# Part of the output projection moved in among the last attention heads

## The chip, the cores and the metric

The kernel runs on one core of a Trainium2 chip. The time is the device time of one execution, in microseconds (us). TensorE (PE) does the matrix products, VectorE (DVE) and ScalarE (ACT) the element-wise work, GpSimd (POOL) some setup and a few transfers, and SyncE (SP) starts nearly all loads of weights. Each engine runs its own instructions in order; they meet at semaphores.

## What is computed

Two transformer blocks in a row, 256 tokens of width 2048, all in float32. The change is in the first block, between its attention and its first residual:

```python
h = rmsnorm(x, pre_mix_g[l])
proj = h @ w_in[l]
...
o_a = swa_sink_attention(...)        # 16 heads of 64: the sliding half
o_b = forgetting_attention(...)      # 16 heads of 64: the forgetting half
o_a = rmsnorm(o_a.reshape(B, S, D_SWA), grp_swa_g[l])
o_b = rmsnorm(o_b.reshape(B, S, D_FOX), grp_fox_g[l])
mix = jnp.concatenate([o_a, o_b], axis=-1) @ w_out[l]
x = x + rmsnorm(mix, post_mix_g[l])
```

The two halves of the attention output are normalised apart. So the first 1024 rows of `w_out` need only the sliding heads, and the other 1024 rows need the forgetting heads.

## The kernel before

**Weights.** Every weight matrix is cut into groups of 512 output columns, and a group into pieces of 256 rows by 512 columns (`PLAN` lists the groups and how many pieces each has). SP loads a piece into one of four slots of `raw`. A function `split` on ACT copies it rounded into `w_hi`, then `split` on DVE writes the difference into `w_lo`. TensorE multiplies each piece three times (`three`: high by high, high by low, low by high), so a piece costs 12 matmuls of 512 columns, or 24 of 256. `group` on ACT and DVE splits three pieces ahead of the one that TensorE multiplies.

**Banks.** PSUM has eight banks of 512 columns. The sums of a group lie in banks 0 and 1 or in banks 2 and 3, in turn; banks 4 to 7 ("upper") serve the attention heads. `banks_free` counts the emptied ones.

**Heads.** There are 32 heads: 0 to 15 sliding, 16 to 31 forgetting. They run as a pipeline of steps `head(i)`. In step i TensorE computes the scores of head i, turns the probabilities of head i-2 and multiplies those of head i-3 with the values. DVE adds the bias and takes the row maximum of head i, then the reciprocal for head i-1, then scales the output of head i-3 into `work`. ACT copies the turned probabilities of head i-2 and takes the exponentials of head i. Steps 0 to 23 lie between the pieces of groups 3 to 8 of the input projection. Steps 24 to 34 follow alone:

```python
for i in range(24, 2 * NH + 3):
    head(i)
stay_warm(4, 16)
phase(1, work, 6, 4)
with pe.Fori(0, 2) as i:
    for e in range(2):
        group(GROUP["w_out"][e], "tok", i, 16, first=1 if e == 0 else None)
```

**From heads to projection.** After the last step the squares of the two halves are summed, and their roots taken together on ACT (`root`, which needs another function table than the exponentials). DVE scales the first 1536 columns of `work` and ACT the other 512. Then `phase(1)` turns `work` into columns: 32 transposes on TensorE in eight quads, a rounded copy per 128 rows on ACT (`hT_hi`) and the difference on DVE (`hT_lo`). Sixteen idle matmuls (`stay_warm`) stand ahead. Only then come the four groups of the output projection, 8 pieces each. `w_hi` has 64 spare columns: pieces whose weights are the stationary operand (input projection, `w_up`) are put 16 columns further in (`PIECE_AT`); the first three of `w_up` are not, since the loop over `w_out` puts them in its own place.

## Time and profile before

| what | value |
|---|---|
| three runs | 1681.15, 1681.36 and 1685.89 us; median 1681.36 |
| the profiled execution | 1682.97 us |
| its span, first to last instruction | 1680.9 us |
| TensorE busy | 1644.2 us, 98% |
| VectorE busy | 1007.8 us, 60% |
| ScalarE busy | 877.3 us, 52% |
| steps 24 to 34, first to last matmul | 250.82 to 271.79 us from the start |
| output projection, first matmul to the end of the last | 281.07 to 368.24 us |

The profiled execution is 1.61 us above the median, and 2.07 us of its time lie outside the span. All places in the trace below are in us from the start of the span.

### The profile page before, as it was taken

The numbers are of one execution on the slowest core, as the hardware profiler recorded it, in microseconds if no ns is written. First come the engines' busy times: TensorE is split into PE (matmuls) and PEld (weight loads), VectorE is DVE, ScalarE is ACT, GpSimd is POOL, SyncE is SP. The second block draws the span as 40 slices with busy tenths as digits, with TensorE's granted clock in tenths as the row PEclk, the third lists the DMA queues.
The fourth block names the chain that finished last, engine by engine and source line by source line (L and its number), as shares of the span: only waits on it lengthen the run. The fifth ranks groups of instructions, "written<-read, shape, count | busy, mean of one in ns | idle before, by whom it ended". The sixth has DMA issues, their size and how long they took to land.

```text
span 1680.9 us, 28894 instructions
## 1 busy us (share of the span) xinstructions
PE 1644.2 (98%) x11198; PEld 1501.7 (89%) x11198; DVE 1007.8 (60%) x1437; ACT 877.3 (52%) x1264; POOL 21.8 (1%) x46
## 2 busy tenths in 40 slices
PE   8999999999999999999999999989999999999996
PEld 8989998879999999999998888878998888898885
DVE  5566667556666666666664444473666455776565
ACT  6355557446555554554453444354434695655455
POOL 3000000000000000000000000010000000000000
PEclk9999999999999999999999999999999999999999
DMA  7654541554666666666665665556566547655641
GB/s 232 203 157 140 162 139 45 193 163 153 192 189 188 187 193 200 200 199 190 197 213 177 200 205 189 175 149 169 166 180 176 162 147 245 185 176 176 195 155 64
DMA packets 154574, 295.09 MB, mean 176 GB/s; under 512 B 13428, under 2 KB 15624, under 8 KB 153592
## 3 DMA queue, kind: packets, MB, share of 16 engines
q1 hardware_dynamic: 153512, 289.76, 55.7%
q0 software_dynamic: 944, 4.14, 0.7%
q8 instruction: 59, 0.97, 0.2%
q14 instruction: 27, 0.22, 0.0%
q10 hardware_dynamic: 32, 0.01, 0.0%
HBM read 291.51 MB, written 2.10 MB: 175 GB/s over the span
## 4 chain that ended last, share of the span: by engine, by line
PE 95%; DVE 2%; ACT 1%; issue 0%; DMA 0%; ACTq 0%; SPq 0%; DVEq 0%
PE bank L1487 29%; PE bank L1489 29%; PE bank L1488 29%; PE upper L1629 1%; PE upper L1632 1%; ACT junk L522 1%; PE upper L1543 1%; PE bank L1543 1%; PE upper L1646 1%; PE upper L1762 1%; DMA x_tok<-in_x 0%; PE upper L1659 0%; PE upper L1660 0%; PE upper L1806 0%; PE upper L1658 0%
## 5 line engine op out<-in xcount | busy, mean ns | idle before, releaser
L891 DVE TENSOR_TENSOR w_lo<-raw,w_hi 128x1024 fp32r<-128x1024 f32 (+1 forms) x548 | 654.5, 1209 | 530.5 <-ACT w_hi L464 529.0
L464 ACT ACTIVATE w_hi<-raw 128x1024 fp32r<-128x1024 f32 (+1 forms) x548 | 568.3, 1049 | 573.4 <-PE bank L1489 567.4
L1487 PE MATMUL bank<-hT_hi,w_hi 128*128 128x256 f32 x2272 | 632.0, 278 | 1.3 <-DVE hT_lo L922 1.3
L1488 PE MATMUL bank<-hT_lo,w_hi 128*128 128x256 f32 x2272 | 629.1, 277 | 0.0
L1489 PE MATMUL bank<-hT_hi,w_lo 128*128 128x256 f32 x2272 | 629.0, 277 | 0.0
L1487 PEld LDWEIGHTS bank<-hT_hi,w_hi 128*128 128x128 f32 x2272 | 427.0, 188 | 2.6 <-issue 1.7
L1488 PEld LDWEIGHTS bank<-hT_lo,w_hi 128*128 128x128 f32 x2272 | 427.5, 188 | 0.0
L1489 PEld LDWEIGHTS bank<-hT_hi,w_lo 128*128 128x128 f32 x2272 | 426.8, 188 | 0.0
L1487 PE MATMUL bank<-w_hi,hT_hi 128*128 128x512 f32 x672 | 264.7, 394 | 0.0
L1489 PE MATMUL bank<-w_hi,hT_lo 128*128 128x512 f32 x672 | 261.8, 390 | 0.0
L1488 PE MATMUL bank<-w_lo,hT_hi 128*128 128x512 f32 x672 | 261.5, 389 | 0.0
L1489 PEld LDWEIGHTS bank<-w_hi,hT_lo 128*128 128x128 f32 x672 | 126.1, 188 | 26.5
L1487 PEld LDWEIGHTS bank<-w_hi,hT_hi 128*128 128x128 f32 x672 | 126.2, 188 | 25.9 <-issue 0.3
L1488 PEld LDWEIGHTS bank<-w_lo,hT_hi 128*128 128x128 f32 x672 | 126.3, 188 | 25.5
L1489 PE MATMUL bank<-w_hi,g_lo 128*128 128x512 f32 x352 | 137.0, 389 | 0.0
L1488 PE MATMUL bank<-w_lo,g_hi 128*128 128x512 f32 x352 | 137.0, 389 | 0.0
L1487 PE MATMUL bank<-w_hi,g_hi 128*128 128x512 f32 x352 | 136.9, 389 | 0.0
L1487 PEld LDWEIGHTS bank<-w_hi,g_hi 128*128 128x128 f32 x352 | 66.1, 188 | 13.8
L1488 PEld LDWEIGHTS bank<-w_lo,g_hi 128*128 128x128 f32 x352 | 66.1, 188 | 13.8
L1489 PEld LDWEIGHTS bank<-w_hi,g_lo 128*128 128x128 f32 x352 | 66.1, 188 | 13.5
L1128 DVE SCALAR_TENSOR_TENSOR cv_gate<-bank,coef,cv_gate 128x255 f32<-128x255 f32 (+1 forms) x88 | 36.4, 476 | 27.3 <-ACT cv_gate L653 26.9
L1128 DVE SCALAR_TENSOR_TENSOR cv_val<-bank,coef,cv_val 128x255 f32<-128x255 f32 (+1 forms) x88 | 36.4, 476 | 26.5 <-ACT cv_val L653 26.1
(347 smaller groups left out, 1080.1 us busy)
## 6 DMA issues: line engine op xcount, KB each, us to landing
raw<-in_w_in SPq DMA_DIRECT2D x180, 512.0 KB, 3.8
raw<-in_w_up SPq DMA_DIRECT2D x176, 512.0 KB, 4.5
raw<-in_w_down SPq DMA_DIRECT2D x80, 512.0 KB, 4.6
raw<-in_w_out SPq DMA_DIRECT2D x64, 512.0 KB, 4.3
raw<-in_w_xkv SPq DMA_DIRECT2D x16, 512.0 KB, 4.5
raw<-in_w_down SPq DMA_DIRECT2D x16, 256.0 KB, 3.1
raw<-in_w_xq SPq DMA_DIRECT2D x8, 512.0 KB, 3.9
raw<-in_w_xo SPq DMA_DIRECT2D x8, 512.0 KB, 4.6
```

The lines of the kernel that those rows point to most:

```text
L464: act.activation(w_hi[:, s, at:at + n], raw[:, s, 0:n], ACT.Copy).then_inc(hi_ready, 1)
L522: act.activation(jk, src, ACT.Square, accum_out=col).then_inc(done, 1)
L891: dve.tensor_tensor(w_lo[:, s, at:at + n], raw[:, s, 0:n], w_hi[:, s, at:at + n].bitcast(F32), ALU.subtract).then_inc(lo_ready, 1)
L1128: ins = dve.scalar_tensor_tensor(out=cv[:, ft, back:S], in0=ps[:, 0:S - back], scalar=coef[:, e, tap, ft:ft + 1], in1=cv[:, ft, back:S], o ...
L1487: pe.matmul(o, l_hi, r_hi, start=start, stop=False, skip_group_check=True)
L1488: pe.matmul(o, l_hi, r_lo, start=False, stop=False, skip_group_check=True)
L1489: return pe.matmul(o, l_lo, r_hi, start=False, stop=stop, skip_group_check=True)
L1543: ins = pe.transpose(bank[pair_bank(n, q)][:, c % 2 * S + b * P:c % 2 * S + (b + 1) * P], src[:, b, c * P:(c + 1) * P], ident[:, :])
L1629: ins = pe.matmul(o[:, lo:hi], qaT[:, h // 2, b * P:(b + 1) * P], ka2[:, h // 8, h % 2, 0:n], start=True, stop=True)
L1632: pe.matmul(o[:, lo:hi], qbT[:, h // 2, b * P:(b + 1) * P], kbT[:, h // 2, h % 2, 0:n], start=True, stop=False)
L1646: ins = pe.transpose(bank[6][:, c * P:(c + 1) * P], probs[:, s, c * P:(c + 1) * P], ident[:, :])
L1762: ins = pe.matmul(bank[4 + 2 * b + h % 2][:, t * P:(t + 1) * P], src[po:po + HD, 1, t, b * P:(b + 1) * P], src[po:po + HD, 0, t, qb * P:(q ...
```

## The change

The four groups of `w_out` are taken apart. Rows 0 to 1023 of the first two groups (`w_out_a`, 4 pieces each, eight in all) run early: one piece after each of the steps 25, 26, 27, 28, 31 and 33 (`EARLY`), and two after step 34. Their sums stay in banks 0 to 3. Then rows 1024 to 2047 of the same two groups (`w_out_b`) are added to them, and the last two groups (`w_out`) follow whole.

For this the sliding half is normalised by itself. Step 22 gets the root on ACT, step 23 the scaling of 1024 columns on DVE, and after step 24 comes the first half of the transposes (`out_phase`), with its copies into new tensors `sT_hi` and `sT_lo`. The forgetting half has the second `out_phase`, after the early pieces. The 16 `stay_warm` matmuls go. The gain that is needed from the first emptied bank on (`mix_gain`) lies in a new place that is free only after the scores of the last head, and its load waits for them. The loops over `w_out` are written out, and the first three pieces of `w_up` now lie 16 columns in, like the rest of `w_up`.

```diff
-    + [("w_out", 8)] * 4 + [("w_up", 8)] * 22 + [("w_down", 24)] * 4
+    + [("w_out_a", 4)] * 2 + [("w_out_b", 4)] * 2 + [("w_out", 8)] * 2 + [("w_up", 8)] * 22 + [("w_down", 24)] * 4
...
+EARLY = (25, 26, 27, 28, 31, 33)
...
-for _name, _before in (("w_up", "w_out"), ("w_down", "w_up"), ("xq", "w_out2")):
+for _name, _before in (("w_down", "w_up"), ("xq", "w_out2")):
...
+    if n == 1:
+        return [p, p + 1, 2 - p, 3 - p, 4, 5, 6, 7][q]
...
+        _, sT_hi, sT_lo = region([("sT_after", [P, NB, D], F32), ("sT_hi", [P, 8, S], F32R), ("sT_lo", [P, 8, S], F32R)])
+        _, mix_gain = region([("mix_gain_after", [P, 11776], F32), ("mix_gain", [P, D], F32)])
...
-            with sp.Fori(0, 2) as i:
-                for e in range(2):
-                    group(A["w_out"][0], i * (2 * W) + e * W, GROUP["w_out"][e], i, 16)
+            w_out = A["w_out"][0]
+            for e in range(2):
+                group(w_out[0:D // 2, :], e * W, GROUP["w_out_a"][e], pieces=(2,) * 4)
+            for e in range(2):
+                group(w_out[D // 2:D, :], e * W, GROUP["w_out_b"][e], pieces=(2,) * 4)
+            for e in range(2):
+                group(w_out, (2 + e) * W, GROUP["w_out"][e])
...
+            pool.wait_ge(scores_done, 2 * NH)
             pool.dma_start(mix_gain[:, :], A["post_mix_g"][0].partition_broadcast(P)).then_inc(gain_loaded, 16)
...
+                if i == 22:
+                    act.wait_ge(swa_mean, 1)
+                    act.activation(half_stat(0), half_stat(0), ACT.Sqrt).then_inc(swa_root, 1)
...
+            early = FIRST_PIECE[GROUP["w_out_a"][0]]
             for i in range(24, 2 * NH + 3):
                 head(i)
-            root(2, 1, mean_ready, root_ready, 4)
+                if i == 24:
+                    out_phase(range(8))
+                if i in EARLY:
+                    split(early + EARLY.index(i) + SLOTS - 1)
+            act.wait_ge(mean_ready, 2)
+            act.activation(half_stat(1), half_stat(1), ACT.Sqrt).then_inc(root_ready, 1)
             scale_part(work, work, 2, head_factor)
-            phase(1)
+            out_phase(range(8, KC))
+            for j in (6, 7):
+                split(early + j + SLOTS - 1)
...
+                if i == 22:
+                    dve.wait_ge(squares, 4)
+                    dve.tensor_scalar(half_stat(0), half_stat(0), 1.0 / D_SWA, EPS, ALU.mult, ALU.add).then_inc(swa_mean, 1)
+                if i == 23:
+                    dve.wait_ge(swa_root, 1)
+                    dve.reciprocal(half_stat(0), half_stat(0)).then_inc(swa_rstd, 1)
+                    dve.wait_ge(swa_rstd, 1)
+                    for c in range(2):
+                        for b in range(NB):
+                            dve.tensor_scalar(work[:, b, c * W:(c + 1) * W], work[:, b, c * W:(c + 1) * W], head_factor(b, c), None,
+                                              ALU.mult).then_inc(scaled, 1)
...
+            def out_piece(g, j, k0):
+
+                u, pair = FIRST_PIECE[g] + j, 2 * (g % 2)
+                pe.wait_ge(lo_ready, u + 1)
+                hi, lo = wide(w_hi, u % SLOTS, 2, W), wide(w_lo, u % SLOTS, 2, W)
+                for c in range(2):
+                    k = k0 + 2 * j + c
+                    pe.wait_ge(loT_done, KC + max(k + 1, 4))
+                    a_hi, a_lo = out_t(k)
+                    for b in range(NB):
+                        ins = three(bank[pair + b][:, :], a_hi[:, b * P:(b + 1) * P], a_lo[:, b * P:(b + 1) * P],
+                                    hi[:, c, :], lo[:, c, :], k == 0, k == KC - 1)
+                ins.then_inc(mm_done, 1)
+
             for i in range(24, 2 * NH + 3):
                 head(i)
-            stay_warm(4, 16)
-            phase(1, work, 6, 4)
-            with pe.Fori(0, 2) as i:
-                for e in range(2):
-                    group(GROUP["w_out"][e], "tok", i, 16, first=1 if e == 0 else None)
+                if i == 24:
+                    out_phase(range(4))
+                if i in EARLY:
+                    j = EARLY.index(i)
+                    out_piece(GROUP["w_out_a"][j // 4], j % 4, 0)
+            for j in (6, 7):
+                out_piece(GROUP["w_out_a"][j // 4], j % 4, 0)
+            out_phase(range(4, 8))
+            for g in GROUP["w_out_b"]:
+                for j in range(4):
+                    out_piece(g, j, 8)
+            for g in GROUP["w_out"]:
+                pe.wait_ge(banks_free, evacuated(g - 2))
+                for j in range(8):
+                    out_piece(g, j, 0)
```

How instructions move on TensorE, at step 24. Before, `head(25)` (its scores, `upper<-kbT,qbT`) followed the values of `head(24)` (`upper<-vb,probsT`) directly:

```order
L1658 MATMUL upper<-vb,probsT 128x64 [waits out_done,probsT_copied]
L1659 MATMUL upper<-vb,probsT 128x64
L1660 MATMUL upper<-vb,probsT 128x64
L1632 MATMUL upper<-kbT,qbT 128x128 [waits biased_done]
L1635 MATMUL upper<-cT2,eye2 128x128
L1632 MATMUL upper<-kbT,qbT 128x256
```

Now 16 transposes stand between them, of the sliding half, into banks 2, 3, 0 and 1:

```order
L1736 MATMUL upper<-vb,probsT 128x64 [waits out_done,probsT_copied]
L1737 MATMUL upper<-vb,probsT 128x64
L1738 MATMUL upper<-vb,probsT 128x64
L1786 MATMUL bank2<-ident,work 128x128 [waits scaled,banks_free]
L1786 MATMUL bank2<-ident,work 128x128 x3
L1786 MATMUL bank3<-ident,work 128x128 x4
L1786 MATMUL bank0<-ident,work 128x128 [waits scaled]
L1786 MATMUL bank0<-ident,work 128x128 x3
L1786 MATMUL bank1<-ident,work 128x128 x4
L1710 MATMUL upper<-kbT,qbT 128x128 [waits biased_done]
```

They wait for `scaled`, the scaling on DVE. Behind the next step stands the first early piece, which waits for `loT_done`, the copies of those transposes on DVE:

```order
L1736 MATMUL upper<-vb,probsT 128x64 [waits out_done,probsT_copied]
L1737 MATMUL upper<-vb,probsT 128x64
L1738 MATMUL upper<-vb,probsT 128x64
L1565 MATMUL bank2<-w_hi,sT_hi 128x512 [waits loT_done,lo_ready]
L1566 MATMUL bank2<-w_lo,sT_hi 128x512
L1567 MATMUL bank2<-w_hi,sT_lo 128x512
```

On ScalarE, the end of step 22 and the start of step 23: two loads of the function table and a root (`stat<-stat`, waits `swa_mean`) are new here; ahead of them are the exponentials of head 22, between them a split and the two copies of group 8 (`kbT`):

```order
L586 ACTIVATE probs,stat<-biased,stat 128x256
L604 ACT_TABLE_LOAD
L604 ACTIVATE stat<-stat 128x2 [waits swa_mean]
L489 ACTIVATE w_hi<-raw 128x1024 [waits mm_done,raw_loaded2]
L634 ACTIVATE kbT<-bank0 64x2x256 [waits k_cleared,mm_done]
L635 ACTIVATE kbT<-bank0 64x2x256
L571 ACTIVATE probsT<-upper 128x384 [waits pv_done,probs_T]
L583 ACT_TABLE_LOAD [waits recip_done,probs_T]
L583 ACTIVATE stat<-stat 128x2 [waits neg_max]
```

So the split now stands behind a table load and the root. The second table load waits for nothing new; the exponential behind it waits for `neg_max`, as before.

On VectorE, the end of step 23: the reciprocal that waits for `swa_root` and the four scalings behind it are new, between the output of head 20 and the bias of head 24:

```order
L1056 RECIPROCAL stat<-stat 128x2 [waits out_done,exp_done]
L1061 TENSOR_TENSOR work<-upper,stat 128x2x64 [waits recip_done,pv_done]
L1076 RECIPROCAL stat<-stat 128x2 [waits swa_root]
L1080 TENSOR_SCALAR work<-work,stat 128x512 [waits swa_rstd]
L1080 TENSOR_SCALAR work<-work,stat 128x512 x3
L1033 SCALAR_TENSOR_TENSOR biased<-upper,c8,foxm 128x128 [waits exp_done,scores_done]
```

## Rows read from the trace of the kernel before

**Rows 1.** The page: busy time of each engine

```profile
PE 1644.2 (98%) x11198; PEld 1501.7 (89%) x11198; DVE 1007.8 (60%) x1437; ACT 877.3 (52%) x1264; POOL 21.8 (1%) x46
```

**Rows 2.** The page: the chain that ended last, by engine

```profile
PE 95%; DVE 2%; ACT 1%; issue 0%; DMA 0%; ACTq 0%; SPq 0%; DVEq 0%
```

**Rows 3.** Timeline of TensorE, 248 to 277 (start, length, line, operands, count)

```profile
248.99 0.39 PE L1632 MATMUL upper<-kbT,qbT 128*128 128x128 f32 x2
...
249.88 0.49 PE L1646 MATMUL upper<-ident,probs 128*128 128x128 f32 x3
...
250.82 0.44 PE L1632 MATMUL upper<-kbT,qbT 128*128 128x128 f32 x2
...
267.53 0.52 PE L1646 MATMUL upper<-ident,probs 128*128 128x128 f32 x3 [0.33 <-ACT probsT L546]
...
271.79 1.91 PE L1550 MATMUL upper<-ones 128*128 128x256 bf16 x16
275.93 1.09 PE L1543 MATMUL bank<-ident,work 128*128 128x128 f32 x8 [2.23 <-DVE work L945]
```

**Rows 4.** Timeline of TensorE, first projection matmul and what follows the last

```profile
281.07 0.47 PE L1487 MATMUL bank<-w_hi,hT_hi 128*128 128x512 f32 x1
...
368.24 1.05 PE L1550 MATMUL upper<-ones 128*128 128x256 bf16 x8
```

**Rows 5.** Busy time by stretch: the transposes (columns as engines, then clock)

```profile
278.00:280.00 2.00, 2.00 (x11) 2.00 (x10) 2.00 (x6) 2.00 (x7) 0.00 (x0) 0.50 0.00 0
```

**Rows 6.** Timeline of TensorE: the transposes of a later normalisation

```profile
1609.63 1.09 PE L1543 MATMUL bank<-ident,mem_tok 128*128 128x128 f32 x8 [2.37 <-DVE mem_tok L945]
1610.56 1.91 PE L1543 MATMUL upper<-ident,mem_tok 128*128 128x128 f32 x16
1612.30 1.04 PE L1543 MATMUL bank<-ident,mem_tok 128*128 128x128 f32 x8
```

**Rows 7.** Timeline of VectorE, 247 to 280

```profile
247.64 1.23 DVE L891 TENSOR_TENSOR w_lo<-raw,w_hi 128x1024 fp32r<-128x1024 f32 x1 [1.80 <-ACT w_hi L464]
...
250.61 0.74 DVE L987 SCALAR_TENSOR_TENSOR biased<-upper,c,foxm 128x128 f32<-128x128 f32 x2
...
252.22 0.29 DVE L1015 TENSOR_TENSOR work<-upper,stat 128x128 f32<-128x128 f32 x1
...
275.00 2.47 DVE L945 TENSOR_SCALAR work<-work,stat 128x512 f32<-128x512 f32 x6
277.50 1.66 DVE L922 SCALAR_TENSOR_TENSOR hT_lo<-bank,gains,hT_hi 128x256 fp32r<-128x256 f32 x4
```

**Rows 8.** Timeline of ScalarE, 245 to 280

```profile
245.57 0.20 ACT L558 ACTIVATE stat<-stat 128x2 f32<-128x2 f32 x1 [2.21 <-DVE stat L997]
...
246.56 1.04 ACT L464 ACTIVATE w_hi<-raw 128x1024 fp32r<-128x1024 f32 x1
...
252.24 0.20 ACT L558 ACTIVATE stat<-stat 128x2 f32<-128x2 f32 x1 [1.34 <-DVE stat L997]
...
260.97 0.61 ACT L522 ACTIVATE junk<-work 128x512 bf16<-128x512 f32 x1
...
276.63 1.57 ACT L503 ACTIVATE hT_hi<-bank,gains 128x256 fp32r<-128x256 f32 x4 [0.29 <-PE bank L1543]
```

**Rows 9.** Timeline of ScalarE: a switch of its function table

```profile
411.75 1.28 ACT L671 ACT_TABLE_LOAD   x1
413.05 1.06 ACT L671 ACTIVATE cv_gate<-cv_gate 128x1024 f32<-128x1024 f32 x1
```

**Rows 10.** Timeline of ScalarE: splits in the first up-projection group

```profile
391.39 1.06 ACT L464 ACTIVATE w_hi<-raw 128x1024 fp32r<-128x1024 f32 x1 [1.82 <-PE bank L1489]
...
397.07 1.06 ACT L464 ACTIVATE w_hi<-raw 128x1024 fp32r<-128x1024 f32 x1 [1.79 <-PE bank L1489]
399.79 1.06 ACT L464 ACTIVATE w_hi<-raw 128x1024 fp32r<-128x1024 f32 x1 [1.66 <-PE bank L1489]
```

**Rows 11.** Issues of transfers: the load of the output gain (KB, us to landing)

```profile
mix_gain<-in_post_mix_g POOLq DMA_DIRECT2D x1, 1024.0 KB, 7.6
```

More of the change, by code:

```diff
@@ L70 @@
 TOTAL = FIRST_PIECE[-1]
+EVACUATIONS = [sum(0 if name == "w_out_a" else 2 for name, _ in PLAN[:g]) for g in range(len(PLAN) + 1)]
 DOWN = [2] * 20 + [1] * 4
+EARLY = (25, 26, 27, 28, 31, 33)
 ROOM = 64
@@ L271, in st, with half_stat, out_t @@
             return stat[:, 4 * k:4 * k + n]
+        def half_stat(half):
+            return stat[:, 4:8].rearrange("p (b k) -> p b k", k=2)[:, :, half]
+        def out_t(c):
+            return (sT_hi[:, c, :], sT_lo[:, c, :]) if c < 8 else (hT_hi[:, c, :], hT_lo[:, c, :])
         def head_factor(b, c):
@@ L633, in x_squares @@
                                (junk if k == 3 else junk2)[:, 0:D // 2])
-            with act.Fori(0, 2) as i:
-                for e in range(2):
-                    g = GROUP["w_out"][e]
-                    if e == 0:
-                        act.wait_ge(squares, 10)
-                    group(g, i, 16, take=lambda g=g, e=e: squares_out(g, i, junk, e))
-                    act.wait_ge(banks_free, evacuated(g) + i * 4)
+            act.wait_ge(squares, 10)
+            for e, g in enumerate(GROUP["w_out_b"] + GROUP["w_out"]):
+                group(g, take=lambda g=g, e=e: squares_out(g, 0, junk, e))
+                act.wait_ge(banks_free, evacuated(g))
             root(3, 2, mean_ready, root_ready)
@@ L1096, in _ @@
             dve.wait_ge(gain_loaded, 16)
-            with dve.Fori(0, 2) as i:
-                for e in range(2):
-                    g = GROUP["w_out"][e]
-                    group(g, i, 16, take=lambda g=g, e=e: gained_out(work, mix_gain, g, i, e, e))
+            for e, g in enumerate(GROUP["w_out_b"] + GROUP["w_out"]):
+                group(g, take=lambda g=g, e=e: gained_out(work, mix_gain, g, 0, e, e))
             def residual(n, k, src, m, done):
@@ L1695, in _, with out_phase @@
                 group(g, "T", side=lambda j, n=n: head(8 + 4 * n + j // 2) if j % 2 else None)
+            def out_phase(quads):
+                for q in quads:
+                    if q == 0:
+                        pe.wait_ge(banks_free, evacuated(READER[1] - 1))
+                    if q in (0, 2, 4):
+                        pe.wait_ge(scaled, 6 + 2 * (q // 2) + 2)
+                    if q == 6:
+                        pe.wait_ge(scaled_act, 4)
+                    for c in (2 * q, 2 * q + 1):
+                        for b in range(NB):
+                            ins = pe.transpose(bank[pair_bank(1, q)][:, c % 2 * S + b * P:c % 2 * S + (b + 1) * P],
+                                               work[:, b, c * P:(c + 1) * P], ident[:, :])
+                    ins.then_inc(tr_done, 1)
@@ new lines, in out_piece @@
+            def out_piece(g, j, k0):
[6 more added lines that the diff above has]
+                    a_hi, a_lo = out_t(k)
+                    for b in range(NB):
+                        ins = three(bank[pair + b][:, :], a_hi[:, b * P:(b + 1) * P], a_lo[:, b * P:(b + 1) * P],
+                                    hi[:, c, :], lo[:, c, :], k == 0, k == KC - 1)
+                ins.then_inc(mm_done, 1)
```

49 lines of the change are left out of this document (38 added, 11 removed).

## Prediction

> **What bounds the kernel now.** The page comes first. TensorE is busy for 1644.2 us of the span, VectorE for 1007.8, ScalarE for 877.3 [rows 1], and 95% of the chain that ended last is TensorE [rows 2]. So only time in which TensorE waits, or works at a lower clock, can be won here; work that merely moves along its queue wins nothing. The timeline of TensorE then shows how much of that there is between the first step that the change touches, step 24, and the end of the projection: 250.82 to 368.24 us, 117.42 us [rows 3, 4].
>
> The work in it is known. A step that nothing holds up takes 250.82 - 248.99 = 1.83 us [rows 3]. Steps 24 to 31 make 14.64 us. Steps 32 and 33 have no scores, only the turn and the values, 250.82 - 249.88 = 0.94 us each [rows 3]; step 34 has the values alone, about 0.6. That makes 2.5 us. 32 transposes at full clock take 3.56 us: in a later normalisation 24 of them stand between 1609.63 and 1612.30, 0.111 us each [rows 6]. The projection is 384 matmuls in 368.24 - 281.07 = 87.17 us, 2.72 us a piece [rows 4]. Together 107.9 us, so 9.5 us are slack:
> steps 24 to 31 last until 267.53, 16.71 us, 2.1 too many; steps 32 to 34 last 4.26 us until 271.79, 1.8 too many; from there to the first transpose at 275.93 are 4.14 us in which only idle matmuls run; and the transposes take 5.14 us until 281.07 instead of 3.56, since the clock is at 0.50 in 278 to 280, the 1.2 GHz level [rows 3, 4, 5]. The last term is 1.6 us. That is what the change can win at most; it needs 5.04 us of it to get past 0.3% of the median, about what a measurement of this kernel tells from no change.
>
> **Part by part.** I follow the three engines through their queues, with the durations of the rows, and write down where TensorE waits.
>
> *The root in step 22.* Exponentials of a head take ScalarE from 245.57 to 246.56, then came a split of 1.04 [rows 8]. Now a table load of 1.28 [rows 9] and a root stand between, so the split ends near 249.05 and VectorE's split, which had started at 247.64 and takes 1.23 [rows 7], ends near 250.25. VectorE's copies of group 8 and its bias of step 23, at 250.61 before, come 1.0 late, and so does the scaled output at 252.22 [rows 7]. TensorE's values in step 24 wait for it until 253.5, and step 24 ends at 254.15. The second table load costs nothing: ScalarE idled 1.34 us there, waiting for VectorE's maximum [rows 8], and the load is queued ahead of that wait.
>
> What a table switch costs is the first place where a page of the Trainium skill speaks against the row. The row shows the next function 1.30 us after the start of a load, the load's own 1.28 and nothing behind it [rows 9]. The Trainium skill ("ScalarE: Activation LUTs", What ACT_TABLE_LOAD costs) puts a switch at about 1283 ns for the load and about 1380 ns for a drain. By the page step 24 would end another 1.4 us later and the sum below would be 1685.7; I go by the row.
>
> *Scaling and first transposes.* Six scalings take 2.47 us, 0.41 each [rows 7]. Two of the new four are done near 254.45; the 16 transposes run from there at 0.111 until 256.3 (wait 0.3). VectorE is free for the bias of head 24 only at 255.3.
>
> *The first piece.* It needs four chunks of `sT_lo`. From bias to exponentials are 1.63 us (250.61 to 252.24), the exponentials 0.99 [rows 7, 8]; so ScalarE begins the high copies at 257.9. A pair takes 0.8 (four in 1.57 [rows 8]), and VectorE's low parts follow at 0.4 each (four in 1.66 [rows 7]): the fourth is there at 260.4. TensorE has done step 25 at 256.3 + 1.83 = 258.1. Wait 2.3; the first piece ends at 263.1.
>
> *Steps with a piece.* For TensorE such a step is 1.83 + 2.72 = 4.55 us. But a loop through the other two engines goes beside it. VectorE's split stands behind its bias of the same step and waits for ScalarE's, which stands behind the exponentials, which wait for the bias: 1.63 + 0.99 + 1.04 + 1.23 = 4.9 us (4.83 with VectorE's overlap between neighbours), and 0.61 more in steps 27 and 28, where ScalarE squares half-done outputs [rows 7, 8]. VectorE starts this stretch late (it ends the low parts at 261.5, while TensorE had asked for head 25 at 256.3) and falls back further. Behind its split is queued the bias of the next head and the output three heads back, and TensorE's values wait for that output. During steps 26 to 28 the pieces hide it: 263.1 + 3 x 4.55 = 276.8. In steps 29 and 30 there is no piece. VectorE's split of step 28 ends near 282.4, its output of step 29 near 284.0, and TensorE's values of step 30 end at 284.9 instead of 276.8 + 3.66 = 280.5. Wait 4.5, the largest.
>
> *The end of the heads.* Step 31 and its piece reach 289.5, steps 32 and 33 with a piece 294.6 (waits 0.5 together), step 34 295.2. Two pieces of 2.72 to 300.7 cover the sums, root and scalings of the forgetting half, which took 4.14 [rows 3]; this wait and the idle matmuls are gone. 16 transposes to 302.4, 0.2 for the first pair of copies, a piece to 305.3.
>
> *Piece nine.* ScalarE and VectorE split it only after their eight copies each: high copies end 3.7 after the first transpose, the split 1.04 later, the low part another 1.2: 306.6. Wait 1.3. From there 23 pieces, 62.6 us, with the splits ahead again: the projection ends at 369.15, against 368.24.
>
> *The other edits.* The gain of 1 MB landed 7.6 us after its issue [rows 11]; issued after the last scores, near 286, it is there at 294, and VectorE asks at 308. If it were late, every split of the second half would wait. Written-out loops cost nothing that a row shows. Where the first three `w_up` pieces lie may matter: ScalarE's splits, each released by a finished piece, are 2.84 apart over two of them (391.39 to 397.07) and 2.72 after (397.07 to 399.79) [rows 10]. I take 0.15 for each of three, 0.5 won; the bound below is nothing.
>
> *Sum.* TensorE's waits are now 10.5 us (1.5 in step 24, 0.3, 2.3, 4.5, 0.5, 0.2, 1.3) against 9.5 of slack: 0.9 us later. The same bookkeeping done on the old steps brings the first transpose to 275.05 instead of 275.93, so it is 0.9 short over eleven steps, and I add that. With 0.5 won at `w_up` the sum is +1.3. On the profiled execution of 1682.97 that gives 1684.3, and this is the number I forecast for the median: the 1.6 us by which that execution stands above the median are as much as its slow transposes cost, so the median before has probably no such dip, and against it the change is +2.9, 0.17%.
>
> **The rivals.** *The gaps do fill* (0.20). If the loop of 4.9 us turns out shorter than TensorE's 4.55, or VectorE catches up, the 4.5 of steps 29 and 30 go: 1679.8; without the 0.9 as well, 1678.9. For more than 0.3% nearly all of the 2.3 ahead of the first piece must go too, 1676.6 or less. For it speaks that VectorE is 60% busy over the span [rows 1]; against it, that the loop is made of waits, not of busy time. The Trainium skill ("Perfetto Trace Analysis", Optimization Strategy) says that interleaving regimes with different contended engines may improve performance. In these steps the trace agrees only in part: TensorE has 2.1 us of slack in 16.7.
>
> *The clock falls in the new gaps* (0.18), the case on the other side. TensorE idled 2.23 us ahead of 275.93 and the clock was at its lower level in 278 to 280, which cost 1.6 us; 2.37 us ahead of 1609.63 cost nothing, the transposes behind it ran at 0.111 [rows 3 to 6]. The new schedule has two gaps of this length, 258.1 to 260.4 and inside step 30, with full-rate pieces behind them. One dip gives 1685.9, two 1687.5; it decides the sign beyond 0.3% when both happen, or one and a loop slower than 4.9.
>
> *The gain is late* (0.02): if it landed some 20 us after its issue, VectorE's splits would wait up to 6 us, 1690.
>
> The forecast itself, the waits move and the time stays, has 0.60.
>
> **How the numbers follow.** Faster by over 0.3% is below 1676.3: half of the first rival's chance, 0.10. Slower is above 1686.4: most of the second, the third, and a tail of the forecast, 0.19. The rest is 0.71. The range goes from 1678.5, the first rival with all its terms, to 1688, two dips and a little.
>
> **What would show it.** Right: TensorE waits for VectorE's output or for the turned copy in steps 29 and 30, 3 to 6 us together; a wait of about 2 on `sT_lo` ahead of the first early piece and of about 1 on a `w_lo` behind the first piece of the second half; no wait after step 34; VectorE's idle time ahead of its splits there at about 1.9 each, on ScalarE. Wrong: step 29 following without a wait, a period of 4.55 on VectorE, or a projection that ends more than 3 us from 369 to 370. The prediction fails as a whole if something outside this stretch moves, a stage that reads `w_hi` from its new place above all.

## The result and the profile after

The changed kernel takes 1687.76 us (median of seven runs, 1685.63 to 1688.89), the kernel before 1682.43 (seven runs beside them, 1681.15 to 1685.89). The ratio is 1.0027, 95% interval 1.0016 to 1.0039: slower by about 0.3%, and certainly not faster. The ratios here and below weigh all runs and are not those of the medians. Here the means are 1687.48 and 1682.87, 4.6 us apart; the medians are 5.3 us, 0.32%, apart. The profiled execution took 1686.70, with a span of 1684.6 and a mean granted clock of 0.992; before it was 1680.9 at 0.995. So the span grew by 3.7.

The page of the changed kernel, busy time and chain, answers to [rows 1, 2]:

```profile
PE 1646.5 (98%) x11182; PEld 1502.5 (89%) x11182; DVE 1007.3 (60%) x1439; ACT 880.6 (52%) x1267; POOL 21.8 (1%) x46
PE 93%; DVE 4%; ACT 2%; issue 1%; DMA 0%; ACTq 0%; SPq 0%; DVEq 0%
```

TensorE has 16 instructions fewer and is busy for 2.3 us more. It has no more work than before and takes longer for it, which points to the clock. The chain has more of VectorE, so there are waits too. TensorE's timeline in the changed kernel (only rows with a wait, the transposes, and the start of step 31 and of the idle matmuls behind the projection) answers to [rows 3, 4]:

```profile
251.68 0.46 PE L1710 MATMUL upper<-kbT,qbT 128*128 128x128 f32 x2 [0.84 <-DVE kbT L1128]
253.61 0.41 PE L1736 MATMUL upper<-vb,probsT 128*128 128x64 f32 x2 [0.48 <-DVE work L1061]
254.59 1.94 PE L1786 MATMUL bank<-ident,work 128*128 128x128 f32 x16
...
260.42 0.76 PE L1565 MATMUL bank<-w_hi,sT_hi 128*128 128x512 f32 x1 [2.05 <-DVE sT_lo L1142]
...
284.31 0.66 PE L1736 MATMUL upper<-vb,probsT 128*128 128x64 f32 x2 [2.17 <-DVE work L1061]
...
285.62 0.74 PE L1710 MATMUL upper<-kbT,qbT 128*128 128x128 f32 x2
...
306.10 0.47 PE L1565 MATMUL bank<-w_hi,hT_hi 128*128 128x512 f32 x1 [0.23 <-DVE hT_lo L1142]
...
309.89 0.50 PE L1565 MATMUL bank<-w_hi,hT_hi 128*128 128x512 f32 x1 [0.81 <-DVE w_lo L937]
...
372.59 1.05 PE L1628 MATMUL upper<-ones 128*128 128x256 bf16 x8
```

The 2.23 us ahead of the transposes and the idle matmuls are gone. In their place stand a wait ahead of the first early piece, one ahead of the values of step 30 and one at piece nine. The first matmul of the piece lasts 0.76 and the first values 0.66, where at full clock they last 0.47 and 0.41. Busy time by stretch (length, TensorE busy, granted clock, DMA share, GB/s) shows the same in its clock column:

```profile
260.00:262.00 2.00, 1.58 (x4) 0.50 0.00 0
262.00:264.00 2.00, 2.00 (x8) 0.64 0.00 0
264.00:282.00 18.00, 17.86 (x109) 1.00 0.27 89
...
282.00:284.00 2.00, 0.14 (x2) 0.98 0.18 50
284.00:286.00 2.00, 1.69 (x8) 0.50 0.67 216
286.00:288.00 2.00, 2.00 (x9) 0.50 0.00 0
288.00:290.00 2.00, 2.00 (x10) 0.50 0.44 66
290.00:292.00 2.00, 2.00 (x8) 0.82 0.98 401
```

Both new gaps of about 2 us are followed by a fall to the 1.2 GHz level, called a dip below. The first costs its piece 1.4 us (264.65 minus 260.42 is 4.23; the same first piece takes 2.83 in the late-split run below, at full clock). The second lasts until about 290.7, since the slice from 290 to 292 has 0.82. Slice by slice it can cost 0.5 x (1.69 + 2.00 + 2.00) + 0.36 = 3.2 us of the busy time. What it does cost is read from the way to the second transposes: 19.65 from the values of step 30 (284.31 to 303.96). The late-split run takes 17.66 for that, with a wait of 0.82 in it and no dip, so 16.84. That makes 2.8 us; the run with the gaps filled takes 16.79, so 2.9. Against the forecast, place by place:

| | forecast | trace |
|---|---|---|
| values of step 24 | 253.5 | 253.61 |
| transposes done, step 25 begins | 256.3 | 256.37 |
| first piece begins, ends | 260.4, 263.1 | 260.42, 264.65 |
| the piece after step 28 is done | 276.8 | 278.56 |
| values of step 30 are done | 284.9 | 285.62 |
| step 31 and its piece are done | 289.5 | 292.77 |
| second transposes begin | 300.7 | 303.96 |
| piece nine begins | 306.6 | 309.89 |
| projection is done | 369.15, with the correction 370.05 | 372.59 |

The first dip vanished in the wait of step 30, which shrank from 4.5 to 2.17 as TensorE came later: the values start at 284.31, where the forecast has them end at 284.9 after some 0.6. From there the second dip runs through to the end: the second transposes and piece nine come 3.3 us late, 2.8 for the dip and 0.4 because the forecast has only 16.4 for those 16.84.

### The profile page after: what moved, and what is told of

Same layout as the page of the kernel before. It is cut to its first block, busy times and chain, and to the rows that moved or that the text cites. A ratio compares the mean times of both kernels' runs of the same rounds, so it can differ in the third digit from the quotient of the medians.

```text
span 1684.6 us, 28655 instructions
## 1 busy us (share of the span) xinstructions
PE 1646.5 (98%) x11182; PEld 1502.5 (89%) x11182; DVE 1007.3 (60%) x1439; ACT 880.6 (52%) x1267; POOL 21.8 (1%) x46
## 4 chain that ended last, share of the span: by engine, by line
PE 93%; DVE 4%; ACT 2%; issue 1%; DMA 0%; ACTq 0%; SPq 0%; DVEq 0%
PE bank L1565 29%; PE bank L1567 29%; PE bank L1566 29%; PE upper L1707 1%; PE upper L1880 1%; ACT junk L547 1%; PE upper L1724 0%; DVE hT_lo L968 0%; PE bank L1621 0%; DVE w_lo L937 0%; ACT w_hi L489 0%; DMA x_tok<-in_x 0%; PE upper L1621 0%; DVE biased L1033 0%; PE upper L1738 0%
## 5 line engine op out<-in xcount | busy, mean ns | idle before, releaser
L1565 PE MATMUL bank<-w_hi,hT_hi 128*128 128x512 f32 x608 | 240.0, 395 | 1.0 <-DVE w_lo L937 0.8
L1567 PE MATMUL bank<-w_hi,hT_lo 128*128 128x512 f32 x608 | 236.8, 390 | 0.0
L1566 PE MATMUL bank<-w_lo,hT_hi 128*128 128x512 f32 x608 | 236.6, 389 | 0.0
L1565 PEld LDWEIGHTS bank<-w_hi,hT_hi 128*128 128x128 f32 x608 | 114.2, 188 | 25.0 <-DVE w_lo L937 1.2
L1567 PEld LDWEIGHTS bank<-w_hi,hT_lo 128*128 128x128 f32 x608 | 114.1, 188 | 24.1
L1566 PEld LDWEIGHTS bank<-w_lo,hT_hi 128*128 128x128 f32 x608 | 114.2, 188 | 22.9
```

The lines of the kernel that those rows point to most:

```text
L1565: pe.matmul(o, l_hi, r_hi, start=start, stop=False, skip_group_check=True)
L1566: pe.matmul(o, l_hi, r_lo, start=False, stop=False, skip_group_check=True)
L1567: return pe.matmul(o, l_lo, r_hi, start=False, stop=stop, skip_group_check=True)
```

## Experiments

Two lengths compare the traces, since what lies ahead shifts whole traces by up to 0.9 us. They are of one execution each; in one row this execution is not typical (three edits, other places: profiled at 1681.55, 3.0 above its median). *Length* is from the first scores of step 23 to the end of the projection: 119.25 before (248.99 to 368.24) and 123.75 after (248.84 to 372.59). *To step 30* is from the start of the first early piece to the start of the values of step 30: 23.89 after (260.42 to 284.31).

| kernel | length | to step 30 | stretches below full clock | median us (lowest to highest, runs) |
|---|---|---|---|---|
| before | 119.25 | | 276 to 282 | 1682.4 to 1682.8 in the four series |
| before, more idle matmuls | 117.59 | | none | 1681.81 (1680.68 to 1686.74, 11) |
| after | 123.75 | 23.89 | 260 to 264, 284 to 292 | 1687.76 (1685.63 to 1688.89, 7) |
| late split | 117.75 | 19.86 | none | 1683.94 (1682.18 to 1684.91, 10) |
| longer loop | 124.57 | 25.98 | 282 to 290 | 1689.65 (1687.72 to 1690.69, 5) |
| other places | 120.63 | 20.88, a piece fewer | 260 to 266 | 1685.18 (1683.42 to 1686.66, 10) |
| gaps filled | 120.89 | 23.88 | none | 1685.39 (1683.76 to 1688.83, 10) |
| root behind | 122.34 | 23.88 | 282 to 290 | 1685.63 (1685.19 to 1687.82, 10) |
| old place of `w_up` | 122.36 | 23.88 | 260 to 266, 284 to 290 | 1688.76 (1685.38 to 1689.70, 10) |
| three edits | 115.70 | 19.88 | none | 1680.66 (1677.95 to 1683.71, 12) |
| three edits, other places | 114.70 | 17.22, a piece fewer | none | 1678.51 (1677.25 to 1682.97, 8) |
| the same, a gap filled | 114.71 | 17.23, a piece fewer | none | 1677.73 (1677.01 to 1681.02, 11) |

The column *to step 30* is the plainest result. Four kernels that leave the loop of VectorE and ScalarE alone have 23.88 or 23.89 there, with a dip in it or without, with 1.8 us more work for TensorE in it or without. So in this stretch TensorE isn't the one that sets the time.

**VectorE's split one step later.** The theory: VectorE stands idle ahead of its split, because the split is queued behind the bias of the same step, and this makes the loop that holds up step 30.

```diff
-                if i in EARLY:
-                    split(early + EARLY.index(i) + SLOTS - 1)
+                if i - 1 in EARLY:
+                    split(early + EARLY.index(i - 1) + SLOTS - 1)
```

> The changed kernel with one edit: in the steps with a piece VectorE does its split one step later, behind the bias, reciprocal and output of the next head. All work is the same. My theory (the loop bias, exponentials, ScalarE's split, VectorE's split, bias of 4.83 us sets the pace of VectorE in steps 25 to 28, and the lag comes out in steps 29 and 30): VectorE's wait of 1.8 to 2.4 us ahead of each split goes, TensorE's waits in step 30 (2.17 for the output, 0.3 for the turned copy) go, the low clock behind them (284 to 291) goes too, and the projection ends 4 to 7 us earlier than in the changed kernel: about 1681 to 1683 us against 1686.7. The rival (the pace of those steps is set by TensorE, and the waits in step 30 come from where the pieces stand, with none after steps 29 and 30): the wait in step 30 stays over 1.5 us and the time stays within 1 us of 1686.7.

VectorE's splits in the changed kernel, and then with the late split:

```profile
265.44 1.23 DVE L937 TENSOR_TENSOR w_lo<-raw,w_hi 128x1024 fp32r<-128x1024 f32 x1 [1.80 <-ACT w_hi L489]
270.26 1.22 DVE L937 TENSOR_TENSOR w_lo<-raw,w_hi 128x1024 fp32r<-128x1024 f32 x1 [1.79 <-ACT w_hi L489]
275.70 1.23 DVE L937 TENSOR_TENSOR w_lo<-raw,w_hi 128x1024 fp32r<-128x1024 f32 x1 [2.41 <-ACT w_hi L489]
281.14 1.23 DVE L937 TENSOR_TENSOR w_lo<-raw,w_hi 128x1024 fp32r<-128x1024 f32 x1 [2.41 <-ACT w_hi L489]
```

```profile
266.73 1.21 DVE L937 TENSOR_TENSOR w_lo<-raw,w_hi 128x1024 fp32r<-128x1024 f32 x1
271.37 1.22 DVE L937 TENSOR_TENSOR w_lo<-raw,w_hi 128x1024 fp32r<-128x1024 f32 x1
276.01 1.22 DVE L937 TENSOR_TENSOR w_lo<-raw,w_hi 128x1024 fp32r<-128x1024 f32 x1
280.64 1.22 DVE L937 TENSOR_TENSOR w_lo<-raw,w_hi 128x1024 fp32r<-128x1024 f32 x1
```

TensorE in the same run, the values of steps 30 and 31 and the second transposes:

```profile
280.87 0.41 PE L1736 MATMUL upper<-vb,probsT 128*128 128x64 f32 x2
283.81 0.41 PE L1736 MATMUL upper<-vb,probsT 128*128 128x64 f32 x2 [0.82 <-DVE work L1061]
298.53 1.91 PE L1786 MATMUL upper<-ident,work 128*128 128x128 f32 x16
```

The idle time ahead of VectorE's splits is gone and they are 4.64 apart in place of 4.82 and 5.44. That is TensorE's own step: in the changed kernel steps 26 to 29 begin 4.64 apart (264.65 to 278.56). Step 30's values no longer wait, and come 4.0 earlier; 0.82 of wait comes in step 31 instead. No dip follows. The length is 6.0 less, 2.8 of it the dip and 3.2 the loop (4.0 earlier at step 30, 0.8 of it waited for in step 31). The ratio to before is 1.0006 (0.9996 to 1.0016): with these two lines the loss can no longer be told from none. The time itself, 1683.57 in the profiled execution, missed the 1681 to 1683 that I had expected: what lies behind the projection took 2.3 us more than in the changed kernel's trace, in part by a dip near 1610.

**A longer loop.** The counter-test: 0.61 us of work without a reader is put on ScalarE in the loop, none on TensorE.

```diff
+                if i in (25, 26, 27, 28):
+                    if i > 25:
+                        act.wait_ge(extra, i - 25)
+                    act.activation(junk[:, D // 2:D // 2 + W], work[:, 0, 0:W], ACT.Square).then_inc(extra, 1)
                 if i in (27, 28):
```

> After, with one more piece of ScalarE work in each of the steps 25, 26, 27 and 28: a square of 128 x 512 whose result nobody reads (some 0.6 us), queued between the exponentials of the step and ScalarE's split. TensorE has nothing added. The theory says that in these steps the loop from VectorE's bias through ScalarE's exponentials and split to VectorE's split sets the pace, not TensorE: then VectorE's splits, which start 4.82, 5.44 and 5.44 apart in the changed kernel, start 5.4, 6.0 and 6.0 apart, the values of step 30 wait 2.4 longer (4.6 in place of 2.2, or the same 2.4 spread over steps 28 to 30), and the stretch up to the projection's end is 2.4 longer at an equal clock. The rival says that the engines' queues have room there and that TensorE's 4.55 a step sets the pace: then the added 0.6 disappears in ScalarE's idle time, the splits keep their spacing within 0.2, and the end moves by less than 0.6.

VectorE's splits in this kernel:

```profile
265.89 1.23 DVE L942 TENSOR_TENSOR w_lo<-raw,w_hi 128x1024 fp32r<-128x1024 f32 x1 [2.32 <-ACT w_hi L490]
271.24 1.23 DVE L942 TENSOR_TENSOR w_lo<-raw,w_hi 128x1024 fp32r<-128x1024 f32 x1 [2.31 <-ACT w_hi L490]
277.20 1.23 DVE L942 TENSOR_TENSOR w_lo<-raw,w_hi 128x1024 fp32r<-128x1024 f32 x1 [2.93 <-ACT w_hi L490]
283.15 1.23 DVE L942 TENSOR_TENSOR w_lo<-raw,w_hi 128x1024 fp32r<-128x1024 f32 x1 [2.92 <-ACT w_hi L490]
```

They are 5.35, 5.96 and 5.95 apart, 0.5 more each, and the idle time ahead of each grew by the same 0.5 (of neighbouring records of ScalarE some 0.1 overlap, so 0.61 of work is 0.5 of time). Step 30 comes 2.1 later, four times this 0.5, and TensorE waits 0.48, 1.09, 1.47 and 1.82 in steps 28 to 30. That is the theory, with 0.5 for my 0.6. At an equal clock I had expected 2.4 at the end of the projection. The length grew by only 0.8, since the clock falls before 284 here (0.77 in 282 to 284), ahead of the wait of 1.82, so that some 1.3 of the dip lies over idle time. ScalarE and VectorE, 52% and 60% busy by the page, hold up TensorE here: busy shares say nothing of it.

**Other places for the pieces.** Is it the loop, or only that steps 29 and 30 have no piece?

```diff
-EARLY = (25, 26, 27, 28, 31, 33)
+EARLY = (25, 27, 28, 30, 31, 33)
```

> After, with the early pieces behind steps 25, 27, 28, 30, 31 and 33 in place of 25, 26, 27, 28, 31 and 33, and nothing else. The theory says that where the pieces stand tells little while VectorE still makes its split ahead of the next head's bias: the loop of 4.8 is then laid through other steps, the wait ahead of the values of step 30 goes (below 0.5), but waits of about the same sum, 2 to 4.5 us, come in other steps from 27 to 31, and the projection ends within 1.0 of where it ends in the changed kernel at an equal clock. The rival says that the wait was only a matter of two steps in a row without a piece: then no wait over 0.5 is left between steps 26 and 34 and the projection ends 2 to 4 us earlier than in the changed kernel at an equal clock, so that the late split is not needed for most of what it won.

TensorE's waits between its first and its last early piece in this kernel:

```profile
268.36 0.41 PE L1736 MATMUL upper<-vb,probsT 128*128 128x64 f32 x2 [0.52 <-DVE work L1061]
281.04 0.41 PE L1736 MATMUL upper<-vb,probsT 128*128 128x64 f32 x2 [1.29 <-DVE work L1061]
```

The second is still that of step 30's values, where I had expected none; I had put the waits in the wrong steps. Their sum, 1.81, is a little less than 2, and a dip at the first piece that cost 1.6 (260.16 to 264.57 is 4.41, against 2.83) hides more. The length is 120.63. The changed kernel without its second dip would be at 123.75 - 2.8 = 120.95, so places alone win 0.3 at an equal clock, nearly nothing, as the theory said. The median is still 2.6 us better than after: in the trace the wait of 1.29 was not followed by a dip.

**Gaps filled.** TensorE writes the scores of steps 25 and 30 three times, long before VectorE asks for them.

```diff
-                for b, (lo, hi) in enumerate(((0, 128), (128, 384))):
+                for b, (lo, hi) in list(enumerate(((0, 128), (128, 384)))) * (3 if i in (25, 30) else 1):
```

> The changed kernel with extra work: in steps 25 and 30 TensorE writes the scores of the head three times instead of once, into the same bank, with the same result; the count that VectorE waits for comes with the last. That adds 1.8 us of matmuls inside each of the two gaps (2.05 and 2.17 us), where VectorE is busy with other things until long after. Theory (the gaps let the clock fall, and the low clock after the second costs 3.4 us): both gaps shrink to under 0.7 us, the clock stays at 1.00 from 258 to 292, and the projection ends 3 us earlier than in the changed kernel, 1683 to 1684 us, although work was added. Rival: the clock falls by the sparse mix of steps and pieces all the same, then the time stays at 1686 to 1688.

The clock by stretch in this kernel:

```profile
246.00:316.00 70.00, 65.20 (x390) 1.00 0.31 105
```

There is no dip, and the length is 120.89, within 0.1 of the 120.95 worked out above for the changed kernel without its second dip. A wait of 1.55 was left in step 30 beside the added work, more than I had expected: without the first dip TensorE arrives earlier and waits longer for the same output. With the gaps filled the dips are gone too, and the median is 1687.76 - 1685.39 = 2.4 us lower, though not at the 1683 to 1684 that I had expected. For the first gap the trace alone proves little, since without any filling five profiles of eight have no dip behind it.

**The root behind the last split of group 8.**

```diff
-                if i == 22:
-                    act.wait_ge(swa_mean, 1)
-                    act.activation(half_stat(0), half_stat(0), ACT.Sqrt).then_inc(swa_root, 1)
...
+            def swa_root_at(n, j):
+                if n == 3 and j == 6:
+                    act.wait_ge(swa_mean, 1)
+                    act.activation(half_stat(0), half_stat(0), ACT.Sqrt).then_inc(swa_root, 1)
...
-                group(g, side=lambda j, n=n: head(8 + 4 * n + j // 2) if j % 2 else None,
+                group(g, side=lambda j, n=n: head(8 + 4 * n + j // 2) if j % 2 else swa_root_at(n, j),
```

> The changed kernel with one edit: the root of the sliding half stands on ScalarE behind the last split of group 8, not ahead of it. Theory: that split ends 1.4 us earlier, VectorE's copies of group 8 1.0 us earlier, and TensorE starts step 24 without the wait of 0.84 for kbT; the first transposes start 0.9 to 1.0 us earlier, near 253.6. But the lag of VectorE decides what follows, so the wait in step 30 moves with it and the end of the projection comes 0.9 to 1.0 us earlier. Rival: the wait ahead of the first piece, or the one in step 30, grows by what is won (something else sets their end), and nothing is gained at the end of the projection.

What it changes is seen in the changed kernel's ScalarE timeline around the root, which also answers to [rows 9]:

```profile
246.53 1.28 ACT L604 ACT_TABLE_LOAD   x1
247.82 0.20 ACT L604 ACTIVATE stat<-stat 128x2 f32<-128x2 f32 x1
247.93 1.04 ACT L489 ACTIVATE w_hi<-raw 128x1024 fp32r<-128x1024 f32 x1
...
250.77 1.28 ACT L583 ACT_TABLE_LOAD   x1
253.19 0.20 ACT L583 ACTIVATE stat<-stat 128x2 f32<-128x2 f32 x1 [1.14 <-DVE stat L1043]
```

The load takes 1.28, the root begins 1.29 after it, and the split stood behind both; the second load ended 1.14 before the exponentials had their maximum. With the root behind the split the wait on `kbT` is gone and that on `work` stays at 0.40. TensorE then has, at the first piece and at the values of step 30:

```profile
259.89 0.47 PE L1567 MATMUL bank<-w_hi,sT_hi 128*128 128x512 f32 x1 [2.05 <-DVE sT_lo L1144]
283.77 0.66 PE L1738 MATMUL upper<-vb,probsT 128*128 128x64 f32 x2 [2.17 <-DVE work L1063]
```

The first piece begins 10.46 after the start of step 23 (249.43) in place of 11.58, 1.1 earlier. All of it is left at step 30, whose values begin 34.34 after that start in place of 35.47: the loop starts 1.1 earlier and takes as long as before, 23.88. The wait in step 30 is 2.17 again. The new waits ahead of it, 0.31 and 0.95, stand where the changed kernel had its first dip of 1.4, which is absent here; the second dip is there. The length is 1.4 less, 1.1 of it this gain and 0.3 because the second dip begins inside its gap (by 283). So the theory held, and its rival did not.

**The old place of the first `w_up` pieces.**

```diff
-for _name, _before in (("w_down", "w_up"), ("xq", "w_out2")):
+for _name, _before in (("w_up", "w_out"), ("w_down", "w_up"), ("xq", "w_out2")):
```

> The changed kernel with one edit: the first three pieces of w_up lie at the start of their slots again, as in the kernel before, not 16 columns in. Theory: their matmuls of 256 columns stand 0.120 us apart again instead of 0.1133, so that ScalarE's splits there are 2.84 to 2.88 apart instead of 2.72, and the first up-projection group takes 0.4 to 0.5 us longer; nothing else moves. Rival: the spacing was due to something else (the extra small matmul in that group, the copies beside it), and the three pieces stay at 2.72 to 2.75.

ScalarE's splits in `w_up`, each released by a finished piece, in the changed kernel and then in this one (as [rows 10]):

```profile
392.39 1.07 ACT L489 ACTIVATE w_hi<-raw 128x1024 fp32r<-128x1024 f32 x1 [0.72 <-PE bank L1567]
395.12 1.06 ACT L489 ACTIVATE w_hi<-raw 128x1024 fp32r<-128x1024 f32 x1 [1.65 <-PE bank L1567]
397.84 1.06 ACT L489 ACTIVATE w_hi<-raw 128x1024 fp32r<-128x1024 f32 x1 [1.66 <-PE bank L1567]
```

```profile
391.76 1.06 ACT L489 ACTIVATE w_hi<-raw 128x1024 fp32r<-128x1024 f32 x1 [1.01 <-PE bank L1567]
394.64 1.06 ACT L489 ACTIVATE w_hi<-raw 128x1024 fp32r<-128x1024 f32 x1 [1.81 <-PE bank L1567]
397.46 1.06 ACT L489 ACTIVATE w_hi<-raw 128x1024 fp32r<-128x1024 f32 x1 [1.77 <-PE bank L1567]
```

2.73 and 2.72 are the spacings in the changed kernel, 2.88 and 2.82 in this one; the next is 2.85 and 2.86, so nearly the same. The spacings miss the first piece. From the first matmul of `w_up` to the 97th, four pieces later, TensorE takes 11.01 in the changed kernel and 11.58 here, 0.57 more. That is too little for the medians, which are 1.0 apart in scattered runs. And the place isn't the whole cause. The fourth piece lies in the same place in both kernels, and takes 2.75 there and 2.86 here. All three traces with the old place have 11.57 or 11.58 for the four. But of the nine with the new place six have 11.00 to 11.02, and three (late split, other places, and the last run below) have 11.41 or 11.42. So the place itself costs between 0.16 and 0.46 for the three pieces; what makes the rest wasn't found.

**The kernel before with 34 idle matmuls in place of 16.** Did the dip before the change cost it its 1.6 us in most runs?

```diff
-            stay_warm(4, 16)
+            stay_warm(4, 34)
```

> The kernel before with 34 idle matmuls instead of 16 ahead of the transposes, 2.1 us more of them, which fill its gap of 2.23 us. Theory: the clock no longer falls there (0.50 in 278 to 280), the transposes take 3.6 us instead of 5.1, and where the dip occurred 1.6 us are won; as only some executions have it, the median falls by 0 to 1.6 us, and the spread of the runs narrows. Rival: the clock falls in spite of it, or the longest runs come from a dip elsewhere, and nothing moves.

The transposes in this kernel, where [rows 3] has a gap of 2.23:

```profile
275.82 1.09 PE L1543 MATMUL bank<-ident,work 128*128 128x128 f32 x8 [0.27 <-DVE work L945]
276.75 1.91 PE L1543 MATMUL upper<-ident,work 128*128 128x128 f32 x16
```

The clock holds, and the length is 117.59, 1.66 less than in the profiled execution of before. The ratio hardly moved: 1.0004 (0.9995 to 1.0013), medians of 1681.81 and 1682.51, and the spread of the runs is no narrower. The interval allows a gain of at most 0.8 us, half of the 1.66. So at least about half of the runs of the kernel before had no such dip, as the prediction supposed when it compared the profiled execution with the median.

**Three edits together**: the late split, the root behind, and the two splits of the second half ahead of ScalarE's and VectorE's last eight copies.

```diff
-            out_phase(range(8, KC))
             for j in (6, 7):
                 split(early + j + SLOTS - 1)
+            out_phase(range(8, KC))
```

> The changed kernel with three edits that add no work: VectorE's splits one step later (as in the late-split run), the root of the sliding half behind the last split of group 8 (as in the root run), and the two splits behind piece nine ahead of the second eight copies on both engines instead of behind them. Theory: the gains add, since each removes another wait. The waits for kbT (0.84) and for w_lo at piece nine (0.81) go, no clock dip. By the same hand schedule as for the forecast TensorE waits 4.6 us instead of 10.6, and the projection ends 6 us earlier than in a changed kernel without a dip; that is about 1.3 us less than the late-split run gained twice over: 2.2 us ahead of it, near 1681.5 us, 1 us under the kernel before. Rival (the waits are coupled, what is won at step 24 or piece nine is waited for elsewhere): the median stays at 1683 to 1684.

The wait at piece nine, 0.79 with the late split alone, is gone, against 0.14 more at the copies ahead of it (0.38 for 0.24). The length is 115.70, 1.9 less than that of the kernel before without its dip (117.59), and the medians are 1.9 apart too, 1680.66 and 1682.51. The ratio is 0.9994 (0.9985 to 1.0002): not told from the kernel before.

**The same with the other places.**

> As the run with three edits, and the early pieces after steps 25, 27, 28, 30, 31 and 33 instead of 25 to 28, 31 and 33, so that the steps without a piece do not stand side by side. Theory: the output of the previous step is ready when TensorE asks; the hand schedule has 3.6 us of waits, 0.9 less than with the old places, and the largest left is the 2.1 ahead of the first piece: near 1680.5 us. Rival (with the late split the places no longer matter): within 0.5 us of the run with three edits.

TensorE's waits between 245 and 320 in this kernel (us in total, times, longest):

```profile
PE bank L1567 <- DVE sT_lo L1144: 2.1, 1, 2.1
PE upper L1738 <- DVE work L1063: 0.4, 1, 0.4
PE bank L1567 <- DVE hT_lo L1144: 0.4, 1, 0.4
```

Three waits are left. The ratio is 0.9978 (0.9967 to 0.9989): faster than the kernel before by 0.2%, and by the medians 0.5% faster than the changed kernel, which ran in another series. Places that win 0.3 alone win 1.0 in length once the loop is gone.

**The same, with the scores of step 25 written three times**, against the last big gap.

> The fastest variant so far (VectorE's split one step later, the root behind the last split of group 8, both splits of the second half ahead of the second copies, pieces behind steps 25, 27, 28, 30, 31 and 33) with the scores of step 25 written three times: TensorE does 1.8 us of added work in the gap of 2.06 ahead of the first early piece, and nobody waits for it. If that gap sometimes drops the clock, which costs 1 to 3 us when it happens (260 to 265 in the changed kernel), filling it takes some of the scatter away: the median comes out 0 to 1.5 lower than the same variant's 1678.5, with the upper end of its runs below 1682, and no stretch below 0.9 in 255 to 275. If the gap costs nothing (the same gap ran without a dip in four profiles of six), the two medians agree within 1.0. The wait ahead of the first piece falls from 2.06 to below 0.4 either way, and the first piece starts within 0.2 of its former place.

TensorE's first early piece in this kernel:

```profile
259.41 0.47 PE L1567 MATMUL bank<-w_hi,sT_hi 128*128 128x512 f32 x1 [0.28 <-DVE sT_lo L1144]
```

Its length is 114.71 against 114.70: the filling is free and wins nothing by itself. The ratio is 0.9978 (0.9969 to 0.9987), the medians are 0.8 apart. Whether this gap costs anything in some runs stays open.

## Why the prediction came out as it did

**The range and the sign** held, the number less so. 1687.76 lies in the range of 1678.5 to 1688.0 but at its upper end, 3.5 above the 1684.3, and the ratio falls just inside "within 0.3%". Against the median of 1681.36 that it started from, the forecast was 2.9 more; the measured medians are 5.3 apart and the means 4.6. The case that came is not the likeliest one: it is the rival of the clock with two dips, for which I had worked out 1687.5.

**The bookkeeping of waits was right.** Each place in the table above is within about 0.1 of the forecast up to the first piece, and step 30's values are where the loop puts them. One wait was named wrongly: the late split of group 8 holds TensorE first at the scores of step 24 (0.84, on `kbT`, whose copies empty the bank), then at the values (0.48). The two together, 1.3, are what I had as 1.5 on the values alone. Piece nine's wait was 0.8 where I had 1.3. (The seven waits of *Sum* add up to 10.6, not 10.5; the place 369.15 isn't affected.)

**The loop** was the heart of the forecast. The forecast has 23.9 us from the first piece (260.4) to the start of step 30's values (284.9 less 0.6), and 23.88 was measured. Undoing the loop takes 4.0 of it away, 0.5 more in each of its four rounds adds 2.1, filling TensorE's gaps changes nothing. Of the 4.5 that I had TensorE wait there, a part is work: its step with a piece takes 4.64, not 4.55. Without the second dip the changed kernel is at 120.95 (worked out), 120.63 and 120.89 (the runs that had none), the kernel before without its dip at 117.59: 3.0 to 3.4 slower, and 2.5 to 2.8 with the 0.6 won at `w_up`. The forecast had +2.9 against the median, which was right for the kernel without its second dip.

**The correction of 0.9** for the bookkeeping was needed nearly in full. 120.95 is 1.7 above the profiled execution before, where the waits alone gave 0.9. Of the 0.8 between them 0.4 lie between the values of step 30 and the second transposes.

**The term that was mis-sized** is the price of the clock in *The clock falls in the new gaps*: "One dip gives 1685.9, two 1687.5". I had priced each dip at the 1.6 us of [rows 5]. The first cost 1.4, but was hidden by the wait behind it and came to nothing; the second lasted from 284 to 290.7 and cost 2.8. The total was right by accident, two errors that cancel. The chance may also have been too low. I had weighed one gap with a dip against one without. But the gap of 2.17 in step 30 was followed by a dip in all three profiles that have it (after, root behind, old place of `w_up`). Three profiles don't settle a chance.

**The start of `w_up`** is 0.57 shorter in this trace, where I had 0.5 for the places. But 0.11 of it fall in a piece that wasn't moved, and three other traces with the new places are only 0.16 shorter, so the mechanism is shown only in part. **The table load** took 1.28 with nothing behind it. The Trainium skill ("ScalarE: Activation LUTs", What ACT_TABLE_LOAD costs) adds a drain of about 1380 ns; no row here shows one, and the forecast by the row held: the values of step 24 came at 253.61, against 253.5.

**The gain** was never waited for: its load was issued at 287.9 and landed 5.2 us later, and its first reader began at 319.0.

**The signs.** The waits in steps 29 and 30 came to 2.17, below the 3 to 6 that I had named, since the first dip took the rest of them. The projection ended 2.6 behind 370, inside the 3 that would have spoken against the forecast.

The span adds up: 1.7 for the waits against the old slack, 2.8 for the second dip, minus 0.6 at `w_up`, makes 3.9; measured 3.7. What lies behind the projection took between 1311.4 and 1315.3 us in these profiles, so 0.2 is within their scatter. Against the kernel before without its dip the length is 6.2 more, less 0.6 at `w_up` 5.6, and the medians are 5.3 apart.

## What to carry to other kernels

Moving work into a pipelined stretch fills gaps only if the pipeline's own loop is shorter than the step that TensorE is given. Write out the loop through all queues (here bias, exponentials, split, split: 4.8 to 5.4 us against 4.64), not the busy shares. If an operation waits in a queue for something that becomes ready within the same step, queue it one step later: two lines won back here what the whole change had lost, as far as the runs can tell. And where a change makes a gap of about 2 us ahead of dense matmuls, add the dip that may follow (here 1.4 to 2.8 us), and see whether a later wait hides it.

## What the runs showed of the hardware

Gaps of nearly equal length had quite different effects. At the 2.17 in step 30 the clock fell each time, within the gap or right behind it (three profiles), which cost 2.8 us in the changed kernel. Behind the 2.05 ahead of the first piece it fell in three profiles of eight. Behind 1.29 and 1.55 in step 30 it stayed up, but in the longer loop it fell during a wait of 1.47, which stood 1.8 behind one of 1.09. And the gap of 2.37 in [rows 6], which all twelve profiles have, was followed by a dip in six of them (late split, old place of `w_up`, gaps filled, longer loop, three edits, and these with other places) and by none in the other six. So the same gap ahead of the same instructions can go either way. The length of a gap alone does not decide it; what does stays open.

The second and third piece of `w_up`, 24 matmuls of 256 columns each, took 2.88 us each in all three traces with their weights at the start of a slot. With the weights 16 columns further in they took 2.72 in six traces and 2.83 in three, all at a granted clock of 1.00. So the place may matter, but it isn't the only thing that does. Why wasn't tested.
